# Issuing a stage's first loads from the stage in front: retention, both later attentions and three output products

## The reference, cut to what matters

```python
def first_block(x, p, ...):
    a = rms_norm(h, g_mix[i]); proj = a @ w_in[i]             # 1024 x 3072
    oa = diff_attention(qa, ka, va, ...)                      # 4 heads
    ob = neighbourhood_attention(qb, kb, vb, ...)             # 16 heads of 32
    h = h + jnp.concatenate([oa, ob], axis=-1) @ w_out[i]
    h = h + hier_moe(rms_norm(h, g_ffn[i]), ...)
    h = h + rms_norm(p[i] @ w_ple[i], g_ple[i]) * jax.nn.sigmoid(rms_norm(h, g_plg[i]) @ w_plg[i])

def hybrid_layer(x, c_act, norm_g, w_ada, b_ada, w_in, w_out, pos):      # twice
    h = rms_norm_2(x, norm_g) * (1.0 + scale[:, None, :]) + shift[:, None, :]
    proj = h @ w_in                                           # 1024 x 4096
    y_ret = merge_heads(retention(rotary(rq), rotary(rk), rv)) * jax.nn.silu(rg)
    y_sb = merge_heads(stick_breaking(sq, sk, sv)) * jax.nn.silu(sg)
    return x + gate[:, None, :] * (jnp.concatenate([y_ret, y_sb], axis=-1) @ w_out)
```

## Time and profile before

| | |
|---|---|
| median of 3 runs | 3312.04 us (3309.97 to 3313.26) |
| profiled execution | 3316.4 us, span 3314.9 us |
| busy in the profile | PE 87%, PEld 67%, DVE 47%, ACT 37%, POOL 10% |
| DMA | 513.63 MB, mean 155 GB/s |
| TensorE clock granted, mean of the profile | 0.944 of full |
| starts of the stages concerned, by SP's first issue | `na` 542.82, `mix_out` 783.27, `ret0` 2105.71, `stick0` 2173.53, `out0` 2410.47, `ret1` 2893.24, `stick1` 2960.79, `out1` 3195.46 |

### The profile page before, as it was taken

One profiled execution on the slowest core, in us unless ns is written; L12 is line 12 of the kernel. 1 busy time (PEld: TensorE's weight loads), 2 busy tenths in 40 slices (PEclk: granted clock), 3 DMA queues, 4 the chain that ended last, 5 costly groups with the idle time before them and its releaser, 6 DMA issues. The chain is left out here.

```text
span 3314.9 us, 59611 instructions
## 1 busy us (share of the span) xinstructions
PE 2869.3 (87%) x22382; PEld 2221.4 (67%) x22382; DVE 1542.8 (47%) x2941; ACT 1211.7 (37%) x2218; POOL 315.2 (10%) x475
## 2 busy tenths in 40 slices
PE   7998896888769999999589999868888999968878
PEld 6786664666648877778467888744466888764446
DVE  3862786885142222222444411268844421058864
ACT  4332664774031000000433222268823222148851
POOL 0001562000021222221000000000000000000000
PEclk9998997999889999999799999879988999979989
DMA  5223654112459999999653221330054222160025
GB/s 181 76 73 108 201 168 145 38 39 87 155 200 357 377 380 375 378 380 372 204 173 129 101 98 44 119 106 13 1 169 152 99 98 76 40 191 18 9 86 181
DMA packets 227717, 513.63 MB, mean 155 GB/s; under 512 B 27216, under 2 KB 101904, under 8 KB 202864
## 3 DMA queue, kind: packets, MB, share of 16 engines
q1 hardware_dynamic: 201632, 445.52, 37.3%
q0 software_dynamic: 24784, 65.87, 7.3%
q10 hardware_dynamic: 1152, 0.27, 0.0%
HBM read 416.76 MB, written 95.76 MB: 155 GB/s over the span
## 5 line engine op out<-in xcount | busy, mean ns | idle before, releaser
L1227 PE MATMUL ps<-w_up,ex_xT 128*32 128x384 f32 x3072 | 343.9, 489 | 18.1 <-DMA w_up<-in_w_dram 17.1
L558 PE MATMUL ps<-wh,in_xh 128*128 (+1 forms) x896 | 352.1, 393 | 0.0
L559 PE MATMUL ps<-wl,in_xh 128*128 (+1 forms) x896 | 350.1, 391 | 0.0
L560 PE MATMUL ps<-wh,in_xl 128*128 (+1 forms) x896 | 349.9, 391 | 0.0
L1229 PE MATMUL ps<-w_up,ex_xT 128*32 128x128 f32 x3072 | 348.1, 274 | 0.0
L1229 PEld LDWEIGHTS ps<-w_up,ex_xT 128*32 128x32 f32 x3072 | 331.4, 110 | 0.4
L560 PEld LDWEIGHTS ps<-wh,in_xl 128*128 128x128 f32 x896 | 169.1, 189 | 35.7
L558 PEld LDWEIGHTS ps<-wh,in_xh 128*128 128x128 f32 x896 | 169.6, 189 | 35.0
L559 PEld LDWEIGHTS ps<-wl,in_xh 128*128 128x128 f32 x896 | 169.4, 189 | 34.6
L1254 PE MATMUL ps<-w_down,ex_hT 128*32 128x512 f32 (+1 forms) x1536 | 173.7, 491 | 6.6 <-DVE ex_y L1192 2.8
L1256 PE MATMUL ps<-w_down,ex_hT 128*32 128x256 f32 x768 | 173.8, 383 | 0.0
(11 more groups left out here) (405 smaller groups left out, 6459.8 us busy)
## 6 DMA issues: line engine op xcount, KB each, us to landing
w_up<-in_w_dram SPq DMA_DIRECT2D x128, 1024.0 KB
w_down<-in_w_dram SPq DMA_DIRECT2D x64, 1024.0 KB
proj<-in_out SPq DMA_DIRECT2D x112, 256.0 KB, 2.0
da_w_ada<-in_w_ada_dram SPq DMA_DIRECT2D x32, 768.0 KB, 4.5
early<-in_w_in_dram SPq DMA_DIRECT2D x11, 2048.0 KB, 10.6
in_raw<-in_w_in_dram SPq DMA_DIRECT2D x8, 2048.0 KB, 9.0
x<-h POOLq DMA_DIRECT2D x30, 512.0 KB, 4.3
proj<-mix_in_out SPq DMA_DIRECT2D x48, 256.0 KB
```

The costliest lines, as they stand in the source:

```text
L558: pe.matmul(o, xh[:, kt, tok], wb[0], start=(kt == 0), stop=False)
L559: pe.matmul(o, xh[:, kt, tok], wb[1], start=False, stop=False)
L560: last = pe.matmul(o, xl[:, kt, tok], wb[0], start=False, stop=(kt == KT - 1))
L1227: pe.matmul(o[group(g), :], tokens[g], wh[j][:, q, 0:HM], start=first, stop=end)
```

## The change

First loads of a stage are issued by the stage in front, into buffers that outlive the barrier: the static `x` and `rows` buffers, which only the dense stages use otherwise, and three buffers that retention and stick breaking now hold jointly. The semaphores they raise are static too and count up over the layers.

- `na`: its two constants and the first `q`, `k` go out at the end of `da`'s SP stream, ahead of the stores of `att`.
- `ret{l}`: `q`, `k` of head 0 and the four constants go out in `in{l}`, at the start of the chunk in fifth place (`prepare=(4, ...)`), ahead of that chunk's weight load.
- `stick{l}`: `q`, `k` of pair 0, the masks and `v` go out in `ret{l}` behind `load(3)` and ahead of the stores of `y`.
- `mix_out`, `out{l}`: row tiles 0 and 1 go out on SP near the end of `na` and near the start of `stick{l}`, where POOL issued them after the barrier.

```diff
+def load_rows_ahead(engine, k, src, cols):
+    for p in range(2):
+        engine.dma_start(k.x[p][:, 0:cols], src[p * P:(p + 1) * P, 0:cols]).then_inc(k.rows_ahead[p], 16)
+    k.ahead_loads += 1
+def load_retention_first(sp, k, proj, decay, q_decay, k_decay, tile_decay):
+    RET = HR * DR
+    for i in range(2):
+        sp.dma_start(k.ret_raw[i], proj[:, i * RET:i * RET + DR].rearrange("(t p) d -> p t d", p=P)).then_inc(k.ret_loaded[i], 16)
+    sp.dma_start(k.ret_dec, decay).then_inc(k.ret_consts_loaded, 16)
...
+def load_stick_first(sp, k, proj, consts):
+    for i in (1, 0):
+        sp.dma_start(k.stick_raw[i][:], ...).then_inc(k.stick_loaded[i], 16)
+    for i, of in enumerate(consts):
+        sp.dma_start(k.stick_con[:, i, :], of).then_inc(k.stick_con_loaded, 16)
+    sp.dma_start(k.stick_v[:], ...).then_inc(k.stick_v_loaded, 16)
 def dense_phase(...):
             for c in range(stored_chunks):
+                if prepare is not None and c == prepare[0]:
+                    sp.wait_ge(x_ready, NT)
+                    sp.wait_ge(x_turned, NT)
+                    for p in range(2):
+                        sp.wait_ge(stored[p], 16 * (c - 1) * NT // 2)
+                    prepare[1](sp)
                 if c + 2 < C:
...
-                if not begun:
+                if not begun and not rows_ahead:
                     pool.dma_start(x[p][:, 0:NK * P], src[p * P:(p + 1) * P, 0:NK * P]).then_inc(x_loaded[p], 16)
 def diff_attention_phase(...):
+            sp.dma_start(k.na_own[:], neighbour[:, 0:4 * DB_H]).then_inc(k.na_consts_loaded, 16)
+            sp.dma_start(k.na_fold[:], ...).then_inc(k.na_consts_loaded, 16)
+            for i in range(2):
+                sp.dma_start(k.na_raw[i][:], ...).then_inc(k.na_loaded[i], 16)
             for t in range(NT):
                 sp.wait_ge(final, HA * (t + 1))
 def neighbourhood_phase(...):
+            sp.wait_ge(turned, PIECES * QUADS)
+            load_rows_ahead(sp, k, att, DM - QUADS * P)
 def retention_phase(...):
-            load(0)
-            sp.dma_start(dec[:], decay).then_inc(consts_loaded, 16)
...
             sp.dma_start(v[:], part(proj[:, 2 * RET:3 * RET])).then_inc(v_loaded, 16)
...
+            load_stick_first(sp, k, proj, stick_consts)
             for u, (h, a, b) in enumerate(PARTS):
                 sp.wait_ge(y_done, u + 1)
 def stick_breaking_phase(...):
             sp.wait_ge(turned, 4)
             load(1)
             load_early(sp, k, *after)
+            load_rows_ahead(sp, k, y, DM - SB)
```

More of the change, by code:

```diff
@@ L540, in turn @@
                     pe.wait_ge(x_ready, t + 1)
+                elif rows_ahead and t < 2:
+                    pe.wait_ge(k.rows_ahead[p], 16 * ahead_loads)
                 else:
-                    pe.wait_ge(x_loaded[p], 16 * (t // 2 + 1))
+                    pe.wait_ge(x_loaded[p], 16 * (t // 2 + 1 - rows_ahead))
                 if t >= 2:
@@ L1681, in lay_bias, with neighbourhood_phase @@
     pool.wait_ge(laid, 16 * (2 * GRID + 3))
-def neighbourhood_phase(nc, k, proj, consts, after):
+def neighbourhood_phase(nc, k, proj, att, after):
     Q0, K0, V0 = 3 * 512, 4 * 512, 5 * 512
@@ L1692, in neighbourhood_phase @@
         bias = [s.sb(f"bias{i}", [P, 2, OFFS, GRID]) for i in range(2)]
-        raw = [s.sb(f"raw{i}", [P, NT, QC]) for i in range(2)]
+        raw, own, fold = k.na_raw, k.na_own, k.na_fold
         v_even = [s.sb(f"v_even{i}", [P, NT, QC]) for i in range(2)]
@@ L1781, in turn @@
                 i, m = divmod(j, PIECES // 2)
-                if m == 0:
-                    pe.wait_ge(loaded[i], 16 * (q + 1))
+                if m == 0 and isinstance(q, int) and q == 0:
+                    pe.wait_ge(k.na_loaded[i], 16)
+                elif m == 0:
+                    pe.wait_ge(loaded[i], 16 * q)
                 if PIECES * q + j > 1:
@@ L1788, in turn @@
                 last.then_inc(turned, 1)
-            pe.wait_ge(consts_loaded, 32)
+            pe.wait_ge(k.na_consts_loaded, 32)
             for j in range(PIECES):
@@ L1967, with retention_phase @@
 HR, DR = 4, 128
-def retention_phase(nc, k, tag, proj, dst, decay, q_decay, k_decay, tile_decay):
+def retention_phase(nc, k, tag, layer, proj, dst, stick_consts):
     RET = HR * DR
@@ L1973, in retention_phase @@
         s = Scope(nc, tag, stack)
-        raw = [[s.sb(f"raw{i}{p}", [P, NT, DR]) for i in range(2)] for p in range(2)]
+        raw = [k.ret_raw, [s.sb(f"raw{i}", [P, NT, DR]) for i in range(2)]]
         v, g = s.sb("v", [P, NT, RET]), s.sb("g", [P, NT, RET])
@@ L2197, with stick_breaking_phase @@
 Z_TOP = 40.0
-def stick_breaking_phase(nc, k, tag, proj, consts, after):
+def stick_breaking_phase(nc, k, tag, layer, proj, y, after):
     S0, SB = 4 * HR * DR, HS * DS
@@ L2208, in stick_breaking_phase @@
         s_ = Scope(nc, tag, stack)
-        raw = [s_.sb(f"raw{i}", [P, NT, 2 * DS]) for i in range(2)]
-        v = s_.sb("v", [P, NT, SB])
+        raw, v, con = k.stick_raw, k.stick_v, k.stick_con
         q_hi, q_lo, k_hi, k_lo = ([s_.sb(f"{n}{p}", [P, SEQ], R) for p in range(2)] for n in ("q_hi", "q_lo", "k_hi", "k_lo"))
@@ L2276, in load @@
                     sp.dma_start(raw[i][:], part(proj[:, first_col:first_col + 2 * DS])).then_inc(loaded[i], 16)
-            load(0)
-            for i, of in enumerate(consts):
-                sp.dma_start(con[:, i, :], of).then_inc(con_loaded, 16)
-            sp.dma_start(v[:], part(proj[:, S0 + 2 * SB:S0 + 3 * SB])).then_inc(v_loaded, 16)
             sp.wait_ge(turned, 4)
@@ L2573, in build @@
                         gain=mod[l, 1], shift=mod[l, 0], rope=(a["cos_128"], a["sin_128"], DR),
-                        order=[2, 0, 1, 4, 5, 6, 3, 7], begun=True)
+                        order=[2, 0, 1, 4, 5, 6, 3, 7], begun=True, prepare=(4, retention_first))
             joint.close()
-            retention_phase(nc, k, f"ret{l}", proj2, y, a["decay"], a["q_decay"], a["k_decay"], a["tile_decay"])
-            stick_breaking_phase(nc, k, f"stick{l}", proj2, (a["stick_mask"], a["stick_upto"], a["triangle"]),
-                                 after=(a["w_out_2"][l], 0))
+            with ExitStack() as pair:
+                k.stick_raw = [pair.enter_context(nc.sbuf_tensor(f"stick{l}_raw{i}", [P, NT, 2 * DS], F)) for i in range(2)]
+                k.stick_v = pair.enter_context(nc.sbuf_tensor(f"stick{l}_v", [P, NT, HS * DS], F))
+                k.stick_con = pair.enter_context(nc.sbuf_tensor(f"stick{l}_con", [P, 3, P], F))
+                retention_phase(nc, k, f"ret{l}", l, proj2, y, (a["stick_mask"], a["stick_upto"], a["triangle"]))
+                stick_breaking_phase(nc, k, f"stick{l}", l, proj2, y, after=(a["w_out_2"][l], 0))
             if l + 1 < LAYERS:
                 k.w_split = [joint.enter_context(nc.sbuf_tensor(f"{n}_{l}", [P, 2, KT, CH], R)) for n in ("wh", "wl")]
-            dense_phase(nc, k, f"out{l}", y, a["w_out_2"][l], h_out, ["resid"] * 2, resid=h_in, gate=mod[l, 2], turned=k.gT,
+            dense_phase(nc, k, f"out{l}", y, a["w_out_2"][l], h_out, ["resid"] * 2, resid=h_in, gate=mod[l, 2], turned=k.gT, rows_ahead=True,
                         after=(a["w_in_2"][l + 1], 2) if l + 1 < LAYERS else None,
```

74 lines of the change are left out of this document (46 added, 28 removed).

## The result

The changed kernel takes **3293.53 us** (median of 4 runs, 3290.34 to 3295.3) against 3312.65 us for the kernel before, run beside it (4 runs, 3309.97 to 3315.01): 19.1 us less, ratio 0.9941, 95% interval 0.9924 to 0.9959. That is 3.9 us above the 3289.6 forecast and inside the range. The profiled execution took 3295.3 us (span 3293.7) against 3316.4 (3314.9): 21.1 us less, where the sum said 22.4.

The account below looks back on a forecast made before the run. PE is busiest (87%), but stage starts wait serially for first loads behind barriers. Gains of 2.2 + 5.7 + 5.1 + 5.2 + 4.2 = 22.4 us from 3312.0 give 3289.6 us, range 3283 to 3298.

Parts of the forecast that it names:

- Retention: `ret0` and `ret1`: waits for first loads and constants go, `v` lands sooner and is late next; 5.7 and 5.1 us gained.
- a bound of 4.4 to 6.5: Each retention stage: gain between 4.4 us (bytes alone) and 6.5 us (ACT's wait alone).
- The 4.4 us: Retention's queue: 1.57 million bytes taken out ahead of `v`, at 354 GB/s, make it land 4.4 us earlier.
- the next head's `q`: `ret1`: the next head's `q`, `k` bind; 0.2 to 1.2 us of margin plus 4.4 gives 4.6 to 5.6, taken as 5.1.
- One sign: Retention: if right, PE now waits for `v` or `load(1)` by a microsecond or less.
- Stick breaking: `stick0` and `stick1`: ACT's first piece waits only for its table load and PE's turns; 5.2 and 4.2 us gained.
- Neighbourhood attention: `na`: ACT's first piece moves up until POOL's first clear holds it; 2.2 us gained, bounds 0 and 4.4.
- Output products: Three output stages: PE's 9.25 us wait for `x` is worth nothing, since DVE's weight splits end last.
- The rival of the colder start: Output stages: earlier turns let the clock rise 3.6 us later, losing 1.8 us each; total gain 17.0 us, chance 0.13.
- Moved issues: `in{l}` and other stages issuing loads ahead: the added issues, 3.9 us of SP's time in `in{l}`, cost zero.
- A second wait under the first: At the barriers: another hidden engine delay eats half of each gain; 11.2 us saved, 3300.8 us, chance 0.09.
- The slower case: Retention: PE stays at 1.2 GHz through the stage, up to 21 us more each; net +20.6, 3332.6 us, chance 0.03.

Follow-up runs that it names:

- e1: Changed kernel with retention's first loads put back behind the barrier in its own stage: 3302.27 us, ratio 0.9958.
- e5: Changed kernel with loads of the same size, read by nobody, put back ahead of `v` in retention: 3304.97 us, ratio 0.9962.
- e9: The changed kernel run once more as it is, on one chip beside e10: 3292.02 us, ratio 0.9933.
- e7: Changed kernel with POOL clearing `na`'s first two buffers in four pieces each and taking over DVE's clear: 3281.11 us, ratio 0.9903.
- e3: Changed kernel with the first row tiles of the three output products loaded by POOL after the barrier again: 3291.02 us, ratio 0.9928.
- e10: The kernel of e7 run once more, on one chip beside e9: 3281.21 us, ratio 0.9908.
- e6: Changed kernel with retention's `v` also loaded one stage earlier, into the weight buffer free in `in{l}`: 3288.48 us, ratio 0.9919.
- e8: Changed kernel with the edits of e6 and e7 together: 3286.95 us, ratio 0.9902.
- e2: Changed kernel with stick breaking's first loads put back behind the barrier in its own stage: 3301.84 us, ratio 0.996.

## Why the prediction was right, and where its sizes were off

**Retention (5.7 and 5.1 forecast, 6.3 and 6.5 measured).** The step was right: `v` decides, ACT's 6.5 us are not all to be had, and a bound of 4.4 to 6.5 held. The time to the first product with `v` fell by 5.79 us in `ret0` (14.77 to 8.98), which is the 5.7; in `ret1` by 5.94 (14.85, from 2893.24 to 2908.09, to 8.91), where 5.1 was taken. The 4.4 us were put down to 1.57 million bytes at 354 GB/s, which put `v`'s landing at 2114.8, 9.1 us after the stage's start; it landed after 8.9. In the rows the difference looks otherwise: 3.89 us of sooner issue (2105.71 to 2109.60) and 0.7 us of shorter flight (9.6 to 8.9). But that split doesn't say what the issues cost by themselves. In the six stages of before, e1 and e5, with the 1.5 MB in front, `v` is issued 2.6 to 4.1 us after the stage's first row and lands after 12.8 to 13.5: what is issued sooner flies longer (10.2 us in `ret1` of e5). So the landing goes mostly by the bytes, as forecast. One thing was mis-stated: in `ret1` the next head's `q` was to bind with a margin of its own. It was issued 4.1 us sooner after the stage's start (4.56 before, 0.45 now) and its flight shortened as well, from a median of 11.2 to 10.8 us, so it kept pace. The remaining 0.5 us in each stage came behind these loads, at a granted clock of 0.87 and 0.88 instead of 0.80 and 0.79 over the stage.

One sign was stated too narrowly, that PE would wait for `v` by a microsecond or less. It did here, by 0.60 and 0.47 us, with PE at the 1.2 GHz level up to that wait; in e9, at 2.4 GHz, it waited 2.91 and 2.79 us, in stages of the same length.

**Stick breaking (5.2 and 4.2 forecast, 3.3 and 3.3 measured).** The term that failed is the step from ACT's first piece to the stage's end. The piece moved by 5.17 us (6.47 to 1.30) and 4.19 us (5.49, from 2960.80 to 2966.29, to 1.30), just as forecast. The forecast then took it for granted that the chain keeps the lead. ACT does keep it in `stick0`: its rows run 5.3 us ahead of those before until the granted clock falls for a short while, near 2280 us. Windows of `stick0`, after:

```profile
2210.00:2280.00 70.00, 60.20 (x323) 33.91 (x321) 60.29 (x90) 58.67 (x87) 0.00 (x0) 0.99 0.11 31
2280.00:2287.00 7.00, 6.94 (x29) 3.94 (x27) 4.36 (x8) 3.89 (x8) 0.00 (x0) 0.59 0.01 2
```

At 1.00 PE, DVE and ACT share the time, each busy 84 to 86% of it. In the 7 us at 0.59 PE is busy throughout and ACT and DVE only 56 and 62% of it: the chain is PE's there, and that dip cost 1.07 us of the lead. A second one, from 2336 to 2342 us at 0.63, cost about as much. In `stick1` the lead went elsewhere: of 4.2 us it lost 1.1 within the first ten, where PE was at 1.2 GHz after the change and already partly at 2.4 before. PE's first products there, before and after:

```profile
2970.49 0.33 PE L2309 MATMUL ps<-stick_q_hi,stick_k_hi 64*128 64x128 f32 x2 [1.57 <-DVE stick_q_lo L2441]
```

```profile
2948.02 0.47 PE L2347 MATMUL ps<-stick_q_hi,stick_k_hi 64*128 64x128 f32 x2 [1.68 <-DVE stick_q_lo L2479]
```

From this row to the first product with `stick_hi` it is 4.00 us before (to 2974.49) and 5.24 after (to 2953.26). Windows over the whole of both stages, before and after:

```profile
2173.54:2410.50 236.96, 196.31 (x960) 108.31 (x960) 185.37 (x264) 184.56 (x262) 0.00 (x0) 0.91 0.12 37
2961.16:3195.80 234.64, 194.62 (x960) 106.86 (x960) 185.27 (x264) 184.65 (x262) 0.00 (x0) 0.92 0.12 37
```

```profile
2165.00:2398.70 233.70, 199.31 (x960) 110.99 (x961) 185.40 (x264) 184.71 (x262) 0.00 (x0) 0.90 0.08 25
2942.66:3174.00 231.34, 195.32 (x960) 108.08 (x960) 185.31 (x264) 184.54 (x261) 0.00 (x0) 0.93 0.08 26
```

DVE and ACT do the same work to within 0.2 us in all four; PE's busy time varies by 4.7 us with the clock. Over all profiles the same order holds. With the loads ahead the stage took 233.2 to 233.7 us at a clock of 0.90 or 0.91 (four stages), 230.3 to 232.2 at 0.92 or 0.93 (fourteen) and 231.2 at 0.94 (two). Without them it took 236.9 and 236.5 at 0.91, 234.7 at 0.92 and 234.8 at 0.94. At like clocks that is about 3 to 3.6 us; over all, the 20 stages with the loads ahead average 231.8 us and the four without 235.7, 3.9 us a stage, where 4.7 was the mean forecast. The forecast needed a discount for a chain that is PE's when the clock is low, or the scatter of 3.4 us in its range. Why the clock fell where it did is not explained: the profiled executions differ in it from one kernel to the next.

**Neighbourhood attention (2.2 forecast, 2.0 measured).** The piece moved from 5.75 to 3.61 us, by 2.14, and POOL's clear is what it waits for, as forecast; e7 shows that this was the next wait.

**Output products (0).** Right for the reason given; the first product stands at 10.99 us both times, and e3 finds nothing. The rival of the colder start falls. In `out0` PE reached 0.40 us a product 6.0 us after the first (2409.67 to 2415.67), against 5.3 us before (2421.46 to 2426.75), which is 0.7 us later and not 3.6; and even that is scatter. Over all output stages the full rate comes 3.3 to 6.1 us after the first product in the 30 with the rows ahead, and 4.7 to 6.1 us in the six without (before and e3). The rule cited for the rival (the Trainium skill, TensorE: Matmul & The Clock Gate, Part 1) says that the rate follows how busy the array was just before; it does not tell these two cases apart, since PE's first product takes 0.80 us, the lower level, in both.

**Moved issues (0).** Right: SP's six issues take from 1928.77 to 1932.52, the next store follows at 1933.92, and `in{l}` lasts 374.1 us with them (after) and 374.1 and 374.2 without (e1).

**The other rivals.** A second wait under the first: in `na` it exists and had its price in the sum; in `ret0` PE, ACT and SP start within 0.04 us of each other. The slower case: it would have needed the 1.2 GHz level through retention; the clock was at 1.00 in the window from 2112 us, 8.5 us after the stage's start, sooner than before. Its condition never came near.

## What to carry to other kernels

At a barrier, a stage's first load is a wait with nothing beside it, and loading it one stage earlier is worth at most what the rows say: the first piece's distance from the stage's start, less whatever is late next (here `v` in the queue, then a memset), less what a lower clock takes back of the lead (stick breaking kept 3.3 of 4.7 us). Move the queue's head, not only the load that an engine waits for: by the stages of e5, freeing the waiting engine was worth 0.8 us and freeing the queue in front of the next load 5.4. And a wait of 9 us can be worth nothing (e3) while splitting a memset behind a 2 us wait is worth more than it; ask for each what ends last.

## What was not expected of the hardware

An issue of one small load took 2.0 to 2.2 us on ACT in eight profiles and 0.40 us in three, of kernels that differ from them only in other stages; it is the first of the delays that made 5 us in its stage, and an 8 KB packet of the instruction queue moved inside it in the eight and before the stage in the three. A row outside the edit can hold as much as the edit itself, and a repeat on one chip (e9, e10) was needed to tell it from chance.

The granted clock moves single stages by as much as the change does, but only where PE's own chain is what ends last. `ret1` in e6 took 57.2 us at a clock of 0.92 and 60.7 in e8 at 0.82, with the same loads ahead; the changed kernel in e9 had 0.92 too and took 60.8, since there PE waited 2.79 us for `v`. `na` with the same program up to there took 234.4 us in e7 and 238.5 in e8. No edit here controls the clock, and no run shows what sets it at a stage's start. So a difference of 3 us between two single profiles is not enough by itself; the same order over many profiles, a row that shows the wait, or the medians (of e1, e2, e5, e9 and e10) have to stand beside it.
